# A decoder step on one core: convolved channels projected first, state scan beside the prompt projections, keys turned in place

## The chip, the core and the metric

One core of one Trainium2 chip runs the whole kernel. The metric is device time of one execution, in us. Seven units matter: TensorE (PE; its weight loads are shown as PEld), VectorE (DVE), ScalarE (ACT), GpSimd (POOL), SyncE (SP, which here only issues DMAs), and the 16 DMA engines. The program is written with explicit semaphores: each engine has one list of instructions, in program order, and waits where it is told to.

## The reference

One decoder layer, for 256 prompt tokens and for 32 sample tokens (8 batches of 4), all in float32:

```
h = rmsnorm(x); q | k | v | z | dt | x,B,C = h @ W_in          # 1024 -> 3080
q, k = rotated norms; attention: three dilated windows, combined   (prompt: own keys;
       samples: 640 of the 1024 cached keys and values per batch, and the new ones)
u = silu(conv4(x,B,C)); dt = softplus(dt + bias)
y = state-space scan over two chunks of 128 (samples: one chunk, start state from the cache)
x += [attention | rmsnorm(y * silu(z))] @ W_out
x += softmax(q_mem . k_mem) v_mem @ W_mo                       # 256 memory rows
x += top-4-of-32 experts, gated, 1024 -> 2048 -> 1024
```

Besides x, the step returns the new keys, values, convolution tails, scan states and memory keys and values.

## The kernel before

The weights go through `ring`, six slots of 128x4096 floats, in the order of the list `UNITS`; unit u uses slot u mod 6. SyncE walks the list, and before unit u waits until the unit six places earlier is used up (`wait_freed`). Cached keys and values are units too (K0 to K7, V0 to V7), as are the cached states (`h0`) and a scratch slot for their transposes. `arena` is a hand-laid scratch memory whose views (`XP`, `UT`, `QK`, `SS`, ...) overlap in time. PSUM has eight banks, named by number.

TensorE's list, which sets the order of everything (lines of the profile in brackets):

1. Turn the normed rows (L336); project q, k, v, z for two prompt tiles (L362: eight outputs, one bank each); the sample rows of all four (L369, four column groups side by side); dt (L377); x,B,C, eight blocks of 128 channels (L389). ScalarE copies each out of PSUM; VectorE norms and rotates q and k (`head_norm`, `rope`) and then convolves, ScalarE applies silu.
2. Turn q and k (L399, L407), the convolution tails (L415); prompt scores (L426); turn the convolved channels (`xb`, L454); running sums of dt (L443 to L448); turn the prompt's probabilities (L463) and weigh the values (L474).
3. The scan, for chunks 0 and 1 and the samples: scores and running sums (L511, L517), the cached states turned four at a time (L497), the carried part (L528, L538), the part within a chunk (L544), the chunk's state (L552). Between them VectorE builds the decay (L1198 to L1212) with an exponential on ScalarE (L1683). GpSimd multiplies the cached states by their decay (L1890). Then eight matmuls add to the cached states (L568), one at a time with VectorE (L1259), and y is turned (L582).
4. Window attention of the samples, for two groups of four batches. Each group goes as two pairs: turn 2x5 key tiles (L601; three PSUM banks, ScalarE copies them to `KTB`, L1699), scores of the pair (L622). After two pairs: max on VectorE, exponential on ScalarE (L1702), turn (L629), values (L642), then token selection (L648).
5. W_out projection (L662, L667) with the residual on VectorE; the memory rows normed and turned (L690); memory keys and values (L704); and so on through the memory attention, its projection, the router, and the experts (L872 to L945), which run in a loop of 16 pairs with their weights in the same ring plus one spare buffer (`SPARE`).

Around L704, w_mem_k is a ring unit; the rows that it multiplies are `HMT`, written by VectorE (L1331).

The first expert's units follow the front's last ones into their slots: `load_expert` (L2016), in the order of slots 0, 1, 2, 4, 5, spare, 3.

## Time and profile before

| | us |
|---|---|
| median of 3 runs | 1406.85 (1405.76 to 1408.14) |
| the profiled execution, by the same clock as the runs | 1409.51 |
| its span, first to last instruction | 1407.3 |
| PE busy | 1275.6 (91%) |
| DVE busy | 343.7 (24%) |
| ACT busy | 268.3 (19%) |
| POOL busy | 35.0 (2%) |
| DMA moved | 470.19 MB, mean 334 GB/s |

The profile is of one execution. Busy PE time is modelled and isn't PE at its peak; the granted clock (1.0 is full speed, 0.50 is half) stands beside it. Idle time of an engine counts only where another waits for it. The span is divided by the page into 40 slices of 35.2 us.

### The profile page before, as it was taken

The numbers are of one execution on the slowest core, as the hardware profiler recorded it, in microseconds if no ns is written. First come the engines' busy times: TensorE is split into PE (matmuls) and PEld (weight loads), VectorE is DVE, ScalarE is ACT, GpSimd is POOL, SyncE is SP. The second block draws the span as 40 slices with busy tenths as digits, with TensorE's granted clock in tenths as the row PEclk, the third lists the DMA queues.
The fourth block names the chain that finished last, engine by engine and source line by source line (L and its number), as shares of the span: only waits on it lengthen the run. The fifth ranks groups of instructions, "written<-read, shape, count | busy, mean of one in ns | idle before, by whom it ended". The sixth has DMA issues, their size and how long they took to land.

```text
span 1407.3 us, 15596 instructions
## 1 busy us (share of the span) xinstructions
PE 1275.6 (91%) x6333; PEld 519.7 (37%) x6333; DVE 343.7 (24%) x600; ACT 268.3 (19%) x520; POOL 35.0 (2%) x43
## 2 busy tenths in 40 slices
PE   6998788899778899999999999999999999999997
PEld 3467545344534233333323233232332323323232
DVE  1247550132405212212112121131211312113122
ACT  2126223310422110111102111021110211102111
POOL 0011320000000000000000000000000000000000
PEclk9998768999997899999999999999999999999999
DMA  9251028875028499999999999999999999999995
GB/s 343 103 198 49 0 78 317 312 268 203 12 74 344 154 409 432 426 431 426 431 426 431 426 430 427 430 427 430 427 430 427 430 427 431 426 430 427 430 427 217
DMA packets 54621, 470.19 MB, mean 334 GB/s; under 512 B 6417, under 2 KB 6673, under 8 KB 27972
## 3 DMA queue, kind: packets, MB, share of 16 engines
q1 hardware_dynamic: 52852, 463.69, 79.3%
q0 software_dynamic: 1744, 6.14, 1.4%
q8 instruction: 18, 0.29, 0.1%
q14 instruction: 7, 0.06, 0.0%
HBM read 463.94 MB, written 5.88 MB: 334 GB/s over the span
## 4 chain that ended last, share of the span: by engine, by line
PE 62%; DMA 23%; DVE 8%; ACT 6%; issue 1%; SPq 0%; ACTq 0%; DVEq 0%
DMA ring<-in_w_gate_up 23%; PE PS L913 22%; PE PS L945 10%; PE PS L893 5%; PE PS L362 4%; PE PS L662 3%; PE PS L389 2%; PE PS L704 2%; PE PS L622 1%; PE PS L716 1%; ACT arena L1699 1%; PE PS L642 1%; DVE arena L1503 1%; DVE arena L1505 1%; DVE arena L1500 1%
## 5 line engine op out<-in xcount | busy, mean ns | idle before, releaser
L913 PE MATMUL PS<-ring,arena 128*64 128x512 f32 x1792 | 406.2, 596 | 38.6 <-DMA ring<-in_w_gate_up 37.8
L913 PEld LDWEIGHTS PS<-ring,arena 128*64 128x64 f32 x1792 | 125.8, 137 | 307.1 <-issue 233.2
L945 PE MATMUL PS<-ring,arena 128*64 128x512 f32 x1024 | 230.3, 597 | 5.6 <-ACT arena L1817 5.6
L1500 DVE TENSOR_SCALAR arena<-PS 128x512 f32<-128x512 f32 x32 | 22.1, 692 | 425.9 <-PE PS L913 425.9
L1814 ACT ACTIVATE arena<-arena 128x512 f32<-128x512 f32 x32 | 20.1, 629 | 522.6 <-DVE arena L1500 522.6
L945 PEld LDWEIGHTS PS<-ring,arena 128*64 128x64 f32 x1024 | 69.3, 137 | 132.7 <-issue 118.8
L1466 DVE TENSOR_TENSOR X<-X,PS 128x1024 f32<-128x1024 f32 x34 | 41.5, 1221 | 272.2 <-PE PS L893 272.2
L872 PE MATMUL PS<-arena 128*64 128x512 f32 (+1 forms) x396 | 97.5, 610 | 2.2 <-issue 2.2
L893 PE MATMUL PS<-arena 128*64 128x512 f32 x340 | 81.3, 592 | 1.4 <-ACT arena L1824 1.4
L1824 ACT COPY arena<-PS 64x512 f32<-64x512 f32 x64 | 37.1, 580 | 158.5 <-PE PS L945 158.1
L362 PE MATMUL PS<-ring,arena 128*128 128x512 f32 x128 | 56.9, 607 | 1.1 <-DVE arena L1028 1.1
L913 PE MATMUL PS<-arena 128*64 128x512 f32 x256 | 57.6, 592 | 0.0
L872 PEld LDWEIGHTS PS<-arena 128*64 128x64 f32 (+1 forms) x396 | 25.7, 137 | 67.7 <-issue 67.7
L893 PEld LDWEIGHTS PS<-arena 128*64 128x64 f32 x340 | 24.4, 137 | 50.1 <-issue 50.1
L662 PE MATMUL PS<-ring,mixT 128*128 128x512 f32 x96 | 41.7, 594 | 0.0
L362 PEld LDWEIGHTS PS<-ring,arena 128*128 128x128 f32 x128 | 24.8, 194 | 32.5 <-issue 31.3
L837 PE MATMUL PS<-arena 32*64 32x512 f32 x264 | 36.8, 627 | 0.0
L1470 DVE TENSOR_TENSOR X<-PS,X 32x512 f32<-32x512 f32 x34 | 23.2, 682 | 49.4 <-PE PS L893 49.1
L389 PE MATMUL PS<-arena,ring 128*128 128x288 f32 x128 | 33.0, 422 | 0.0
L913 PEld LDWEIGHTS PS<-arena 128*64 128x64 f32 x256 | 18.4, 137 | 36.5 <-issue 36.5
L704 PE MATMUL PS<-ring,arena 128*128 128x512 f32 x64 | 27.7, 593 | 1.5 <-DVE arena L1331 1.5
L1796 ACT COPY arena<-PS 128x512 f32<-128x512 f32 x33 | 19.4, 587 | 47.8 <-PE PS L872 47.8
(325 smaller groups left out, 1028.4 us busy)
## 6 DMA issues: line engine op xcount, KB each, us to landing
ring<-in_w_gate_up SPq DMA_DIRECT2D x112, 2048.0 KB, 24.8
ring<-in_w_down SPq DMA_DIRECT2D x64, 2048.0 KB, 22.5
arena<-in_w_gate_up SPq DMA_DIRECT2D x16, 2048.0 KB, 27.6
ring<-in_w_in SPq DMA_DIRECT2D x6, 2048.0 KB, 17.0
ring<-in_cache_win_k SPq DMA_DIRECT2D x8, 1024.0 KB, 6.9
ring<-in_cache_win_v SPq DMA_DIRECT2D x8, 1024.0 KB, 10.4
ring<-in_w_out SPq DMA_DIRECT2D x2, 2048.0 KB, 13.7
ring<-in_cache_mem_k SPq DMA_DIRECT2D x4, 1024.0 KB, 7.8
```

Of the source, the lines that this page charges most:

```text
L362: last = mm(PS[:, 2 * g + t, :], hT[:, k, t * P:(t + 1) * P], w[:, k, :], start=k == 0, stop=k == KT - 1)
L389: last = mm(PS[:, bank, 0:NTOK], w[:, k, m % 4 * P:(m % 4 + 1) * P], hT[:, k, :], start=k == 0, stop=k == KT - 1)
L662: last = mm(PS[:, 2 * t + half, :], lhs[:, k, t * P:(t + 1) * P], w(k), start=k == 0, stop=k == nk - 1)
L704: last = mm(PS[:, MKV_BANKS[n], :], HMT[:, k, t * P:(t + 1) * P], w[:, k, :], start=k == 0, stop=k == KT - 1)
L837: last = mm(PS[64 * half:64 * half + 64, nb, :], EROW[r, :], BGU[r, half * 512:(half + 1) * 512], start=True, stop=False, tile_position=(N ...
L872: last = mm(PS[64 * half:64 * half + 64, 2, :], SEL[0:m, t, :], XN[0:m, t, half * 512:(half + 1) * 512], start=t == 0, stop=t == 2, tile_p ...
L893: last = mm(PS[64 * part:64 * part + 64, banks[half], :], SW[:, at:at + 64], YB[:, half, :], start=True, stop=True, tile_position=(0, 64 * ...
L913: last = mm(PS[64 * half:64 * half + 64, nb, :], XT[:, k, :], w[:, k % 2, c:c + 512], start=False, stop=k == KT - 1, tile_position=(0, 64 ...
L945: last = mm(PS[64 * half:64 * half + 64, 5, :], AT[:, k % 4, 64 * (k // 4):64 * (k // 4) + 64], w[:, k % 4, half * 512:(half + 1) * 512], ...
L1466: v.tensor_tensor(x, x, PS[0:n, b:b + 2, :], ALU.add).then_inc(sem("scatter_added"), 1)
L1500: v.tensor_scalar(G1.rearrange("q (c b p) -> q c b p", **by_part), gu[:, 0], 7.0, None, ALU.min).then_inc(sem("gate_ready"), 1)
L1824: ins = s.copy(YB[64 * odd:64 * odd + 64, half, :], PS[64 * half:64 * half + 64, 5, :])
```

## The change

It touches the front only (all before the expert loop). Six edits go together:

- **Order of projection.** x,B,C and dt come first, then the sample rows of q, k, v, z, then the eight prompt outputs in the order z0 z1 q0 k0 q1 k1 v0 v1 (`PROMPT_OUTS`), through two banks by turns. `project(i, k0, k1)` does part of one; the parts stand between steps of the scan.
- **The scan** runs before prompt attention and beside these parts. The cached states are turned one at a time through one bank (bank 7), each waiting for ScalarE's copy of the one before. `XD` is gone: dt multiplies `XB` in place, and `start_y` takes the skip term first. GpSimd builds all three `DTRI` before it scales the cached states.
- **Norms of q and k** (`norm_qk`) come after the scan on VectorE; eight state updates follow behind y.
- **Keys in place.** A turned key tile is copied back over the tile it came from; `KTB` is gone. Two banks by turns instead of three. The score matmuls read the four dense tiles of a batch with a stride. A group scores all four batches at once, one column group of 32 each: 48 matmuls a group for four batches.
- **Prompt attention and window attention overlap.** Twenty key tiles (batches 0 to 3) are turned between the steps of prompt attention; window attention's steps stand between the four W_out outputs of the prompt.
- **Loads.** `LOADS` gives SyncE's order, apart from the slots in `UNITS`. Values leave the ring: `VA` are four arena buffers, filled once the scan is over. K units are used up when their group's scores are done. The first expert's units go to slots 0 to 4, the spare, then 5.

```diff
+UNITS = ["z", "q", "k", "v", "xbc0", "xbc1",
+         "K0", "K1", "K2", "K3", "h0", "scratch",
+         "K4", "K5", "K6", "K7", "wout0", "wout1",
+         "wmq", "mem0", "mem1", "wmk", "mem3", "wmv",
+         "pad", "pad", "pad", "mem2", "pad", "wmo"]
+LOADS = ("xbc0 xbc1 z q k v h0 K0 K1 wout1 K2 K3 V0 V1 V2 V3 wout0 K4 K5 K6 K7 V4 V5 V6 V7 "
+         "wmk wmq mem0 mem1 wmv mem3 mem2 wmo").split()
...
+            def turn_state(b):
+                if b == 0:
+                    loaded("h0")
+                    pe.wait_ge(sem("proj_kept"), 3)
+                else:
+                    pe.wait_ge(sem("h0t_kept"), b)
+                for p in range(4):
+                    last = nc.tensor.transpose(PS[:, 7, p * P:(p + 1) * P], H0[:, b, p, :], ident)
+                last.then_inc(sem("h0_turned"), 1)
...
+            project(0, 0, KT)
+            turn_xb(0)
+            turn_xb(1)
...
+            project(1, 0, 4)
+            turn_xb(2)
+            project(1, 4, KT)
...
+            chunk_scores(0)
+            for c in range(4):
+                turn_state(c)
+                if c < 3:
+                    project(2, 2 * c, 2 * c + 2)
+            within(0)
+            chunk_state(0)
+            project(2, 6, KT)
+            chunk_scores(1)
+            for c in range(4):
+                turn_state(4 + c)
+                if c < 3:
+                    project(3, 2 * c, 2 * c + 2)
+            carried(1)
+            within(1)
+            chunk_state(1)
+            project(3, 6, KT)
+            chunk_scores(2)
+            project(4, 0, 5)
+            carried(2)
+            within(2)
+            project(4, 5, KT)
...
+            project(5, 0, KT)
...
+            project(6, 0, 4)
+            pe.wait_ge(sem("state_rows_kept"), 1)
+            turn_qk(0, (2, 3))
+            project(6, 4, KT)
+            project(7, 0, 4)
+            turn_y(0)
+            turn_y(1)
+            project(7, 4, 6)
+            turn_y(2)
+            add_states(0)
+            project(7, 6, KT)
+            add_states(1)
...
+            def turn_keys(n):
+                g, b, j = n // 20, n // 5, n % 5
...
+                if n % 20:
+                    pe.wait_ge(sem("kt_kept"), n - 1)
...
+            for n in range(10):
+                turn_keys(n)
+            turn_probs(0, (0, 1))
+            for n in range(10, 14):
+                turn_keys(n)
+            pe.wait_ge(sem("scores_kept"), 2)
+            weigh_values(0, 2)
+            turn_probs(1, (3, 6, 7, 0))
+            for n in range(14, 18):
+                turn_keys(n)
+            weigh_values(1, 1)
+            for n in range(18, 20):
+                turn_keys(n)
...
+            window_scores(0)
+            pe.wait_ge(sem("att_kept"), 2)
+            loaded("wout0")
+            project_half(mixT, 8, wout[0], 0, WOUT_BANKS[0][0], "mixed_ready")
+            turn_window_probs(0)
+            loaded("wout1")
+            project_half(mixT, 8, wout[1], 0, WOUT_BANKS[0][1], "mixed_ready")
+            weigh_window(0)
+            project_half(mixT, 8, wout[0], 1, WOUT_BANKS[1][0], "mixed_ready")
+            for n in range(20, 40):
+                turn_keys(n)
+            window_scores(1)
+            project_half(mixT, 8, wout[1], 1, WOUT_BANKS[1][1], "mixed_ready")
+            turn_window_probs(1)
+            weigh_window(1)
+            pe.wait_ge(sem("mix_ready"), 1)
+            project_samples(mixT, 8, wout, WOUT_BANKS[2][0], "mixed_ready")
```

ScalarE's list from the first projection copy to the end of prompt attention, whose order the prediction uses:

```diff
+            keep_projected(0)
+            keep_projected(1)
...
+                s.activation(Z[0:n, t, :], Z[0:n, t, :], ACT.Silu).then_inc(sem("z_silu_ready"), 1)
+            act.wait_ge(sem("acum_ready"), 1)
+            s.activation(TOE, DT1, ACT.Exp)
...
+            keep_state(0)
+            keep_state(1)
+            seg_exp(0)
+            keep_state(2)
+            keep_state(3)
+            keep_projected(2)
+            keep_state(4)
+            keep_state(5)
+            seg_exp(1)
+            keep_state(6)
+            keep_state(7)
...
+            for n in range(5):
+                keep_keys(n)
+            prompt_exp(0)
+            for n in range(5, 10):
+                keep_keys(n)
+            prompt_exp(1)
+            act.wait_ge(sem("window_stored"), 64)
+            keep_probs(0, (0, 1))
+            for n in range(10, 14):
+                keep_keys(n)
+            keep_att(0, 2)
+            keep_probs(1, (3, 6, 7, 0))
+            for n in range(14, 18):
+                keep_keys(n)
+            keep_att(1, 1)
+            for n in range(18, 20):
+                keep_keys(n)
```

SyncE's waits for the values:

```diff
+            for i, name in enumerate(LOADS):
+                if name == "V0":
+                    sp.wait_ge(sem("h_updated"), 8)
+                    sp.wait_ge(sem("y_turned_kept"), 3)
+                    sp.wait_ge(sem("qk_normed"), 3)
+                    sp.wait_ge(sem("prompt_state_stored"), 16)
+                elif name == "V4":
+                    sp.wait_ge(sem("att_rows_ready"), 1)
+                elif name[0] != "V" and U[name] >= RING:
+                    wait_freed(U[name])
```

## Rows read from the trace of the kernel before

**Rows 1.** The page's part 2: what the DMA engines moved, by slice of 35.2 us.

```profile
GB/s 343 103 198 49 0 78 317 312 268 203 12 74 344 154 409 432 426 431 426 431 426 431 426 430 427 430 427 430 427 430 427 430 427 431 426 430 427 430 427 217
```

**Rows 2.** Table by stage: window, its length, then busy us by engine, clock, DMA.

```profile
core 0: us, PE busy (x) PEld busy (x) DVE busy (x) ACT busy (x) POOL busy (x), PEclk, DMA share, GB/s
116.70:147.60 30.90, 22.83 (x175) 20.25 (x175) 23.15 (x42) 20.25 (x67) 6.49 (x10) 0.78 0.13 47
147.60:202.90 55.30, 42.66 (x180) 24.74 (x180) 36.73 (x46) 10.62 (x20) 19.79 (x11) 0.67 0.04 12
202.90:277.50 74.60, 61.20 (x477) 36.51 (x476) 6.60 (x18) 25.77 (x51) 0.00 (x0) 0.86 0.83 308
277.50:312.20 34.70, 33.26 (x146) 15.82 (x146) 7.66 (x15) 5.59 (x12) 0.95 (x1) 1.00 0.72 256
312.20:466.35 154.15, 124.44 (x604) 66.56 (x604) 50.07 (x109) 40.39 (x93) 3.04 (x5) 0.87 0.40 156
466.35:1407.30 940.95, 885.71 (x4356) 295.36 (x4356) 183.64 (x294) 137.50 (x224) 0.00 (x0) 1.00 0.97 414
450.00:475.00 25.00, 19.29 (x75) 7.88 (x73) 6.68 (x21) 4.34 (x6) 0.00 (x0) 0.66 0.02 7
```

**Rows 3.** The chain of waits: start, us, what.

```profile
312.23 27.70 PE PS L704 x64
...
709.48 24.83 DMA ring<-in_w_gate_up
```

**Rows 4.** Timeline of SyncE, 400 to 440 us: start, us, engine, line, tensors.

```profile
401.61 18.50 SPq L2016 DMA_DIRECT2D ring<-in_w_gate_up  x3
...
436.93 0.33 SPq L2016 DMA_DIRECT2D ring<-in_w_gate_up  x1
```

**Rows 5.** Table by stage, four us in the state updates.

```profile
188.00:192.00 4.00, 4.00 (x5) 1.44 (x5) 1.42 (x3) 1.84 (x3) 0.85 (x1) 0.50 0.11 34
```

**Rows 6.** Groups by line, PE, 15 to 313 us: busy, mean ns, idle before.

```profile
L362 PE MATMUL PS<-ring,arena 128*128 128x512 f32 x128 | 56.9, 607 | 1.1 <-DVE arena L1028 1.1
L389 PE MATMUL PS<-arena,ring 128*128 128x288 f32 x128 | 33.0, 422 | 0.0
...
L369 PE MATMUL PS<-ring,arena 128*32 128x512 f32 x64 | 7.1, 594 | 0.0
...
L474 PE MATMUL PS<-arena 128*64 128x128 f32 x48 | 6.1, 409 | 3.5 <-ACT arena L1659 3.5
L463 PE MATMUL PS<-CN,arena 128*128 128x128 f32 x24 | 4.5, 360 | 0.0
...
L377 PE MATMUL PS<-WDT,arena 128*128 128x8 f32 (+1 forms) x48 | 4.3, 230 | 0.0
```

**Rows 7.** Timelines of POOL and DVE around the scaling of the states.

```profile
165.96 9.33 POOL L1890 TENSOR_TENSOR ring<-ring,small 128x1024 f32<-128x1024 f32 x4 [13.97 <-PE PS L497]
...
155.06 0.68 DVE L1218 TENSOR_TENSOR arena<-arena,RP 128x512 f32<-128x512 f32 x1
...
168.86 2.38 DVE L1218 TENSOR_TENSOR arena<-arena,RP 128x512 f32<-128x512 f32 x1
```

**Rows 8.** Timelines of ACT and PE: copies of turned keys, and turns of memory keys.

```profile
252.80 4.99 ACT L1699 COPY arena<-PS 128x512 f32<-128x512 f32 x10 [5.43 <-PE PS L601]
...
385.95 1.04 PE L773 MATMUL PS<-CN,ring 128*128 128x128 f32 x8
387.27 1.15 PE L773 MATMUL PS<-CN,ring 128*128 128x128 f32 x8 [0.29 <-ACT arena L1770]
```

**Rows 9.** Groups by line and shape, ACT, 116 to 203 us: the prompt's exponentials.

```profile
L1650 ACT ACTIVATE arena<-arena,small 128x256 f32<-128x256 f32 x8 | 4.0, 495 | 1.5 <-DVE small L1148 1.5
...
L1650 ACT ACTIVATE arena<-arena,small 128x128 f32<-128x128 f32 x8 | 3.1, 388 | 0.4 <-DVE small L1148 0.4
```

**Rows 10.** Groups by line, PE, 203 to 313 us: window attention.

```profile
L601 PE MATMUL PS<-CN,ring 128*128 128x128 f32 x160 | 23.0, 311 | 0.0
L622 PE MATMUL PS<-arena 128*32 128x512 f32 (+2 forms) x192 | 19.0, 354 | 3.2 <-ACT arena L1699 3.2
L642 PE MATMUL PS<-ring,arena 128*32 128x512 f32 x80 | 12.5, 787 | 2.0 <-ACT arena L1707 2.0
```

More of the change, by code:

```diff
@@ L56, in slot_loads @@
 def slot_loads(upto, slot):
-    return sum({"s": 0, "p": 0, "K": 2, "V": 2, "m": 2}.get(UNITS[i][0], 1) for i in range(slot, upto, RING))
+    return sum({"s": 0, "p": 0, "K": 2, "m": 2}.get(UNITS[i][0], 1) for i in range(slot, upto, RING))
 def constants():
@@ new lines, in turn_qk @@
+            def turn_qk(t, banks):
+                pe.wait_ge(sem("qk_normed"), t + 2)
+                for j in range(2):
+                    for p in range(4):
+                        last = nc.tensor.transpose(PS[:, banks[j], p * P:(p + 1) * P],
+                                                   QK[:, t, j, 2 * p:2 * p + 2, :].rearrange("p h d -> p (h d)"),
+                                                   ident)
+                    last.then_inc(sem("qk_turned"), 1)
+            project(6, 0, 4)
@@ new lines, in _ @@
+            pe.wait_ge(sem("state_rows_kept"), 1)
[9 more added lines that the diff above has]
+            add_states(1)
+            add_states(2)
+            add_states(3)
+            pe.wait_ge(sem("proj_kept"), 11)
+            for j in range(2):
+                r = slice(32 * j, 32 * j + 32)
+                for p in range(4):
+                    last = nc.tensor.transpose(PS[:, j, p * NTS:(p + 1) * NTS],
+                                               QKS[r, 2 * p:2 * p + 2, :].rearrange("p h d -> p (h d)"),
+                                               ident[r, r])
@@ new lines, in turn_probs, with weigh_values @@
+            def turn_probs(i, banks):
+                pe.wait_ge(sem("probs_ready"), i + 1)
+                for j in range(i + 1):
+                    for s in range(8):
+                        last = nc.tensor.transpose(PS[:, banks[2 * j + s // 4], s % 4 * P:(s % 4 + 1) * P],
+                                                   SCO[i][s // 4][:, s % 4, j * P:(j + 1) * P], ident)
+                last.then_inc(sem("probs_turned"), 1)
+            def weigh_values(i, bank):
+                pe.wait_ge(sem("probs_kept"), i + 1)
+                for p in range(4):
+                    for e in range(2):
+                        h = 2 * p + e
+                        for j in range(i + 1):
+                            last = mm(PS[64 * e:64 * e + 64, bank, p * P:(p + 1) * P], V[:, j, h * DH:(h + 1) * DH],
+                                      PT[:, j, 4 * e + p, :], start=j == 0, stop=j == i)
+                last.then_inc(sem("att_ready"), 1)
@@ new lines, in _ @@
+            for c in (6, 7):
+                silu_conv(c, slice(0, SEQ), c + 1)
+            for c in range(8):
+                silu_conv(c, slice(SEQ, NTOK), 9)
+            act.wait_ge(sem("proj_ready"), 1)
+            s.copy(QKS[0:64].rearrange("p h d -> p (h d)"), PS[0:64, 7, :]).then_inc(sem("proj_kept"), 1)
+            s.copy(V[0:NTS, 2, :], PS[64:96, 7, :]).then_inc(sem("proj_kept"), 1)
+            s.copy(Z[0:NTS, 2, :], PS[96:128, 7, :]).then_inc(sem("proj_kept"), 1)
+            root_heads(64, AH, DH)
@@ new lines, in _, with keep_qk @@
+            s.copy(HOUT, PS[:, 2, :].rearrange("p (c n) -> p c n", c=4)).then_inc(sem("state_rows_kept"), 1)
+            act.wait_ge(sem("y_gated"), 3)
+            square_y(2)
+            root_heads(P, 2 * AH, DH)
+            act.wait_ge(sem("y_squared"), 3)
+            root(RS, SSQ, 512)
+            keep_projected(5)
+            root_heads(P, 2 * AH, DH)
+            def keep_qk(t, banks):
+                for j in range(2):
+                    act.wait_ge(sem("qk_turned"), 3 * t + j + 1)
+                    s.copy((qT, kT)[j][:, :, t * P:(t + 1) * P],
+                           PS[:, banks[j], :].rearrange("p (c n) -> p c n", c=4)).then_inc(sem("qk_kept"), 1)
@@ L1654, in _, with keep_probs @@
-            for i in range(2):
+            def keep_probs(i, banks):
                 act.wait_ge(sem("probs_turned"), i + 1)
-                banks = (2, 3, 5, 6)
                 for j in range(i + 1):
```

1022 lines of the change are left out of this document (493 added, 529 removed).

## The prediction

> **What bounds the kernel now.** I read the page's 40 slices first [rows 1]. From the fourteenth slice on the DMA engines move some 430 GB/s; before that they have long holes. Two regimes, then. The table by stage puts their border at 466.35 us, the first expert matmul [rows 2]: the expert stage takes 940.95 us with DMA 97% busy, the front 466 us. The chain of waits says who leads in the expert stage: from about 650 us on every pair of experts holds a wait of this form for its weights, thirteen of them up to 1380 us [rows 3]. That stage can only move as a whole. It loads into six ring slots and one spare, so its first loads wait for front tensors: SyncE issues them at 401.61 and the last before the first expert at 436.93 [rows 4], and DMA then stands idle (7 GB/s from 450 to 475 us [rows 2]) until the first expert gives slots back. So a us taken from the front is a us from the end, if the seven units still land before the first expert. Since DMA already idles there, front transfers aren't the bound either.
>
> In the front TensorE leads. Windows 116.7 to 202.9 us (prompt attention, then state scan) are the weak ones [rows 2]: 86.2 us, of which PE is busy 22.83+42.66 = 65.5, at granted clocks 0.78 and 0.67. So 20.7 us are idle, and the work at full clock is 22.83x0.78 + 42.66x0.67 = 46.4 us. The cause is a ping-pong of one short chain: PE waits for VectorE, ScalarE or GpSimd. The windows before it have a PE that never stops. The clock is at 1.2 GHz (0.50) for stretches that follow such gaps [rows 5].
>
> **The change, by stages.** The step everything hangs on is when the first memory projection (L704) starts: 312.2 us now [rows 3]. Nothing of consequence changes after it, so 154.15 + 940.95 us follow as before.
>
> *Stage 1, to the sample projections.* The order is now xbc, dt, samples; the six weight units come in the order xbc0, xbc1, z, q, k, v. 33.0 + 4.3 + 7.1 = 44.4 us from 15.6 [rows 6], ends 60.0. xbc1 is wanted 16.5 us after the start, where k was wanted after 13.7 without a wait. The dt weights move past z, q, k and v on SP's queue to stand right behind xbc1; they could be late by 0 to 3 us, taken 0. The convolution (VectorE) starts on arrival and is hidden by the 4.1 us that PE spends on each block.
>
> *Stage 2, state scan beside the prompt projections, to the first cached key.* PE work: 8 projections of 16 matmul instructions of 0.429 us, 6.87 each = 55 (from 56.9 for 128 [rows 6]). Besides, all of the 65.5 busy us of the two weak windows except the prompt's transposed probabilities and weighted values (4.5 + 6.1 [rows 6]), which belong to stage 3: 54.9 as they ran, or at full clock 46.4 less about 9, 37. Since projections now stand in most gaps, the clock stays mostly high: I take 45, nearer to full clock. That is 100. Waits, laid out instruction by instruction: PE comes to turn_state(1) before ScalarE has done z's silu and the exponentials (which stand behind the copy of projection 1): 1.5 us; turn_state(3) and within(0) stand behind seg_exp(0): 1.6; carried(1): 0.6; the tail of add_states about 1. The old stalls for VectorE in the scan are covered: chunk t's chain on VectorE and ScalarE (four steps on 128x1024 elements, each twice the size of the 0.68 us one in rows 7 and so about 1.2) is some 5 us, and between its matmuls stand 5 to 7 us of projection. VectorE's two long norms (norm_qk: four operations of that size, root and rotation, about 8 us each) have project 5 and 6 over the first, and the rest of 6 and of 7 over the second. 100 + 4 + 2 for clock drops = 106, bounds 96 (37 and 4) to 122 (54.9 and 12 of waits). Ends 166.
>
> GpSimd's scaling of the cached states (4 instructions, 9.33 us) moved behind the last dtri. The VectorE multiply of 0.68 us took 2.38 while it ran [rows 7]. Between the end of chunk 1 and within(2) PE has 1.7 + 1.3 + 4.3 + 3.3 = 10.6 us of its own; VectorE needs about 7, stretched. So cost 0; without cover up to 4. That the third dtri goes ahead of the scaling removes a wait of 2.3 us.
>
> The Trainium skill (SBUF — State Buffer, section "SBUF: two separate sides") has VectorE and GpSimd share one port pair under an exclusive lock, the loser blocked for the whole instruction. The trace agrees with the row above. By that rule the state scaling, four instructions beside chunk 1's VectorE chain, could stretch it by up to 9.3 us; if none of it were covered, the sum would be 9 us higher.
>
> *Stage 3, cached keys 0 to 19 among prompt scores.* All copies are ScalarE's, which leads here. Twenty key copies: 0.50 each with three banks (10 in 4.99), but 0.66 with two, as the memory keys show (two pairs start 1.32 us apart) [rows 8]. The change has two banks and writes a turned key tile back over itself: 13.2. Exponentials 8 x 0.388 + 8 x 0.495 = 7.1 [rows 9], with a table load and the reads of the sums about 8.5; eight further copies at about 0.5, 4.2. Sum 25.9; ScalarE's waits for PE's weighted values and VectorE's probabilities about 5; PE at half clock now and then (a key tile then takes 1.0 us, not 0.5) 2. Taken 33, bounds 26 and 40. Ends 199. The added waits on `window_stored` and `conv_stored` queue ScalarE's and VectorE's following copies behind GpSimd's stores, but those are issued some 10 us ahead: 0.
>
> *Stage 4, window attention among the w_out projections, to L704.* PE was busy 61.20 + 33.26 = 94.5 us from 202.9 to 312.2 [rows 2]. Off go twenty of the forty key turns, half of 23.0, and half of the scores' 19.0, since four batches go as one column group where two groups of two took 4 x 4.75 [rows 10]: 94.5 - 11.5 - 9.5 = 73.5. The twenty key turns left go from 11.5 to 13.3 at the two-bank pace: 75.3, and some 7 less if the 0.86 clock of the first window became 1.0. The waits for the window's exponential go (a projection stands there); those before the values (L642: 2.0 in two [rows 10]) stay, as do the like ones, 1.8, before the token matmuls, and 0.6 comes behind the last key. The end is longer than now: the memory rows' norm stood beside the w_out projections and now comes behind the last attention output (square, root, scale, turn, and the sample rows' four adds ahead of VectorE's copies): 2.6 us. Sum 82.3; taken 80, since more of it will run at full clock; bounds 75 and 90. If four-wide groups ran as two pairs, add 9.5; the value matmuls L642 already run four wide, ten streams of 512 columns in 12.5 us, so I don't expect it.
>
> DMA beside this: V0 to V3 wait on SP for the state update, and wout0, K4 to K7, V4 to V7 and the memory weights stand behind them. At 370 GB/s (308 at a share of 0.83 in the 202.9 to 277.5 window [rows 2]) 5.2 MB take 14 us. wout0 waits for the state store, lands about 190, wanted at 199; K4 to K7 are issued after the first scores at 204, land at 218, wanted at 233; V4 to V7 issued at 225, wanted at 265; w_mem_k, issued at 252, lands at 260, wanted at 279. None ends last. Which front tensor frees each slot changes, so the last expert unit is now a down-projection half, wanted later than gate-up part 3 was: 0.
>
> *Sum.* 60 + 106 + 33 + 80 = 279 for L704, against 312.2: 33 us less. Profiled execution: 1409.5 - 33 = 1376.5 (span 1407.3 - 33 = 1374.3). That execution was 2.7 us above the median of the runs, 1406.85, so the median after is 1374.
>
> **Rivals.** *A, as above*, with its own range 1364 to 1384. *B, PE holds 2.4 GHz and the waits are shorter*: stage sums at their low ends, 60 + 96 + 28 + 77 = 261, or up to 8 more; gain 43 to 51, time 1356 to 1364. For it: from 116.7 to 277.5 us busy time at a clock below 1.0 lost 5 + 14 + 9 = 28 us [rows 2]. Against: ScalarE leads stage 3 whatever PE's clock. *C, the interleave gives half back*: each projection piece is issued between waits in program order, so one late ScalarE instruction holds the projection as well. Ten waits of 1.5 us in place of five, and stages 3 and 4 near their ends (38, 87): gain 12 to 22, time 1385 to 1395. For it: ScalarE's list is strictly ordered and mixes state copies, exponentials and projections. *D, the front isn't worth its time*: weights late for the expert stage, gain under 3. Against: DMA idles before the first expert. Time 1405. *E, slower*: the mechanism is the clock. The new order replaces few long gaps by many of 0.6 to 1.6 us; if these hold PE at 1.2 GHz through stages 2 to 4, their work at full clock (about 92 + 15 + 68 = 175 us) doubles for the part concerned. Half clock for 43 us of work would eat the 33 us and the 10 us of slow clock that the sum contains; above that it's slower, and with 60 us of work at half clock the time is 1406.85 + 17 = 1424. The place would be the scan. For it: 0.67 in the scan now. Against: the 202.9 to 277.5 window has 0.86 with many gaps near 1 us already.
>
> **Chances.** A 0.62, B 0.13, C 0.18, D 0.03, E 0.04. The range with 8 in 10: 1360 to 1391. Measurement tells 0.2%, 2.8 us, from no change: faster 0.93, same 0.03, slower 0.04.
>
> **What would show it.** Right: L704 starts at 270 to 290 us; PE's gaps between 60 and 166 sum to 3 to 9 us and the clock there is above 0.9; the windows' score group is 9.5 us, not 19; the expert stage stays 941 us within 2; first sample projection ends about 60. Wrong: a PE wait over 3 us on ScalarE in the scan; a DMA as releaser anywhere before L704; key tiles above 0.8 us each; the clock below 0.75 between 60 and 166; the expert stage longer by what the front saved.

## The result, and the profile after

The changed kernel takes 1373.34 us (median of 1363.94 to 1375.52, four executions) where the kernel before takes 1406.7 in the same comparison (1405.76 to 1408.14): ratio 0.9749, 95% interval 0.9703 to 0.9795. Forecast were 1374.0 and a range of 1360 to 1391. The profiled execution took 1373.2 us, its span is 1371.2. One of the four was 9 to 12 us faster than the others; the last section comes back to it. One execution of serial_scan (1520.01 us, mean clock 0.825) and one of the kernel before beside it (2197.15 us, 0.554) fell in a slower state and are left out of the times and ratios below.

The table by stage of the changed kernel (window, length, busy us of each engine, clock, DMA), to be laid beside [rows 2]:

```profile
16.28:63.35 47.07, 47.07 (x241) 33.73 (x240) 18.49 (x45) 12.93 (x36) 2.93 (x11) 0.93 0.81 279
63.35:166.58 103.23, 99.96 (x414) 54.45 (x411) 63.21 (x102) 28.77 (x57) 25.40 (x20) 0.93 0.28 96
166.58:198.20 31.62, 20.80 (x155) 17.62 (x153) 9.03 (x13) 23.31 (x61) 0.72 (x1) 0.84 0.79 308
198.20:275.04 76.84, 69.34 (x540) 34.54 (x541) 13.58 (x31) 21.01 (x42) 0.95 (x1) 1.00 0.66 248
275.04:431.00 155.96, 126.80 (x603) 67.82 (x603) 49.88 (x109) 39.57 (x91) 3.03 (x5) 0.85 0.42 157
431.00:1371.20 940.20, 885.50 (x4356) 298.35 (x4356) 183.75 (x294) 137.91 (x225) 0.00 (x0) 1.00 0.98 414
```

Three things are to be seen. The last two rows are nearly those of before (154.15 and 940.95 us; the first expert matmul itself starts at 431.39, which makes them 156.35 and 939.8): whatever was gained was gained ahead of the memory projections (L796, formerly L704), which start at 275.04 instead of 312.23, 37.2 us earlier. Of that 36.1 reach the end of the span. The second row, the state scan with the prompt projections in it, has a PE that is busy 99.96 of 103.23 us; before, the two windows that held the scan and the prompt attention were busy 65.5 of 86.2. And of the four stages that the change rebuilt, the third leaves PE idle most: PE is busy 20.80 of its 31.62 us, ScalarE 23.31.

PE's waits in the second stage, as the view of waits sums them (from 63 to 166 us):

```profile
PE PS L492 <- ACT ring L1763: 2.3, 2, 1.6
PE PS L501 <- ACT ring L1763: 0.8, 1, 0.8
PE PS L524 <- DVE mixT L1306: 0.2, 1, 0.2
```

That is 3.3 us in four waits (in the fences, `PE PS L492 <- ACT ring L1763: 2.3, 2, 1.6` reads: line 492 of PE waited for ScalarE's line 1763, 2.3 us in two waits, the longest 1.6). The window attention's groups of the changed kernel, to be laid beside [rows 10] (PE, 198 to 275 us):

```profile
L652 PE MATMUL PS<-CN,ring 128*128 128x128 f32 x80 | 11.7, 284 | 1.5 <-ACT ring L1825 1.0
L706 PE MATMUL PS<-ring 128*32 128x512 f32 x64 | 7.3, 595 | 1.4 <-ACT ring L1825 1.4
...
L706 PE MATMUL PS<-ring 128*32 128x128 f32 x64 | 2.1, 272 | 0.0
```

With its third shape (1.0 us) L706, the scores of eight batches, is busy 10.4 us where L622 took 19.0. score_pairs, below, tests whether that comes of the four column groups.

### The profile page after: what moved, and what is told of

It reads as the page before. It is cut to its first block, busy times and chain, and to the rows that moved or that the text cites. A ratio compares the mean times of both kernels' runs of the same rounds, so it can differ in the third digit from the quotient of the medians.

```text
span 1371.2 us, 15591 instructions
## 1 busy us (share of the span) xinstructions
PE 1254.9 (92%) x6333; PEld 511.6 (37%) x6333; DVE 344.1 (25%) x606; ACT 270.2 (20%) x520; POOL 33.4 (2%) x43
## 4 chain that ended last, share of the span: by engine, by line
PE 63%; DMA 24%; ACT 6%; DVE 6%; issue 1%; SPq 0%; ACTq 0%; DVEq 0%
DMA ring<-in_w_gate_up 23%; PE PS L1004 23%; PE PS L1036 10%; PE PS L984 5%; PE PS L423 4%; PE PS L744 3%; PE PS L395 3%; PE PS L796 2%; PE PS L808 1%; PE PS L652 1%; DVE arena L1626 1%; DVE arena L1628 1%; DVE arena L1623 1%; PE PS L1025 1%; ACT arena L1989 1%
## 5 line engine op out<-in xcount | busy, mean ns | idle before, releaser
L1004 PE MATMUL PS<-ring,arena 128*64 128x512 f32 x1792 | 406.0, 596 | 35.2 <-DMA ring<-in_w_gate_up 34.4
L1999 ACT COPY arena<-PS 64x512 f32<-64x512 f32 x64 | 37.1, 580 | 159.6 <-PE PS L1036 159.3
L423 PE MATMUL PS<-ring,arena 128*128 128x512 f32 x128 | 58.1, 596 | 0.0
L395 PE MATMUL PS<-arena,ring 128*128 128x288 f32 x128 | 35.2, 441 | 0.0
L652 PE MATMUL PS<-CN,ring 128*128 128x128 f32 x160 | 24.6, 297 | 11.6 <-ACT ring L1825 11.0
L796 PE MATMUL PS<-ring,arena 128*128 128x512 f32 x64 | 29.4, 622 | 2.0 <-DVE arena L1454 2.0
```

Of the source, the lines that this page charges most:

```text
L395: last = mm(PS[:, XBC_BANKS[m], 0:NTOK], w[:, k, m % 4 * P:(m % 4 + 1) * P], hT[:, k, :], start=k == 0, stop=k == KT - 1)
L423: last = mm(PS[:, i % 2, :], hT[:, k, t * P:(t + 1) * P], w[:, k, :], start=k == 0, stop=k == KT - 1)
L652: last = nc.tensor.transpose(PS[:, KT_BANKS[g][n % 2], p * P:(p + 1) * P], K[:, j, p * P:(p + 1) * P], ident)
L796: last = mm(PS[:, MKV_BANKS[n], :], HMT[:, k, t * P:(t + 1) * P], w[:, k, :], start=k == 0, stop=k == KT - 1)
L1004: last = mm(PS[64 * half:64 * half + 64, nb, :], XT[:, k, :], w[:, k % 2, c:c + 512], start=False, stop=k == KT - 1, tile_position=(0, 64 ...
L1999: ins = s.copy(YB[64 * odd:64 * odd + 64, half, :], PS[64 * half:64 * half + 64, 5, :])
```

## Experiments

The same stretch of code is granted 2.4 GHz in some executions and 1.2 GHz in others (last section), and the changed kernel alone spreads over 14 us. So each experiment is read twice: by its ratio to the kernel before, and by the stage of its own profile that it touches. All stages in one table, us, each kernel from the one execution that was profiled; "tails" are the turned convolution tails (L413), the first score is L635, the first window score L706, the memory projections L796 in the changed kernel's lines:

| kernel | tails to first score | to first window score | to memory projections | to first expert | ratio to before, 95% |
|---|---|---|---|---|---|
| changed | 98.45 | 36.40 | 76.84 | 156.35 | 0.9749 (0.9703-0.9795) |
| changed_again | 97.98 | 37.50 | 76.84 | 159.57 | 0.9709 (0.9679-0.9739) |
| serial_scan | 122.57 | 35.37 | 76.86 | 157.20 | 0.9915 (0.9897-0.9933) |
| score_pairs | 98.45 | 36.46 | 87.65 | 153.07 | 0.9784 (0.9759-0.9808) |
| keys_last | 94.06 | 38.69 | 78.55 | 156.33 | 0.9746 (0.9724-0.9768) |
| wout_last | 94.08 | 33.90 | 88.55 | 155.47 | 0.9840 (0.9817-0.9863) |
| three_key_banks | 94.07 | 33.88 | 74.10 | 151.80 | 0.9693 (0.9663-0.9723) |
| states_spread | 105.75 | 36.19 | 77.40 | 151.76 | 0.9786 (0.9759-0.9814) |
| dt_spread | 98.55 | 36.29 | 77.40 | 152.35 | 0.9704 (0.9671-0.9737) |
| no_scaling | 98.36 | 36.83 | 77.39 | 152.40 | 0.9720 (0.9689-0.9752) |
| dve_copies | 98.16 | 36.17 | 79.10 | 151.39 | 0.9744 (0.9719-0.9769) |
| mem_first | 94.06 | 36.57 | 75.05 | 155.45 | 0.9719 (0.9686-0.9752) |
| best | 99.01 | 32.79 | 74.99 | 152.40 | 0.9695 (0.9670-0.9719) |

**serial_scan: the projections in a block ahead of the scan.**

```
             project(1, 4, KT)
+            for i in range(2, 8):
+                project(i, 0, KT)
...
             for c in range(4):
                 turn_state(c)
-                if c < 3:
-                    project(2, 2 * c, 2 * c + 2)
```

> The six projections that stand in pieces inside the state scan go ahead of it as one block, their copies and VectorE's two head norms beside them; the scan then runs alone. Theory (the gain is the filling of the scan's gaps): PE's waits in the scan come back. Per chunk VectorE's and ScalarE's four steps take about 5.5 us with one or two state turns left beside them, so about 3 us of wait for each of three chunks, 4 to 5 us for the norm of y behind the last, and some 8 us of half clock: 15 to 25 us more than the changed kernel, 1388 to 1398 us, with the clock in the scan below 0.85. Rival (the gain comes from the other stages and from convolving first, and the interleave is worth little): less than 5 us more, 1373 to 1378.

Measured: 1395.91 us, 22.6 above the changed kernel's first median and 29.5 above its second (changed_again, below). Its stage is 24.1 us longer than the profiled changed kernel's (28.5 longer than that of executions that had full clock there), the stages behind it are the same within 1.1 us. The table by stage of this kernel, and PE's waits in the stage:

```profile
61.87:184.44 122.57, 111.19 (x383) 61.34 (x379) 57.84 (x97) 31.57 (x60) 23.41 (x19) 0.80 0.21 74
```

```profile
PE PS L494 <- ACT ring L1751: 5.7, 6, 2.2
PE PS L578 <- DVE arena L1334: 3.1, 1, 3.1
PE PS L526 <- DVE mixT L1296: 1.1, 1, 1.1
```

The theory stands in its size and the rival falls, but the theory's parts don't: the waits are 11.4 us (with two of 0.8 and 0.7), only 8 more than with the interleave, where I had expected some 14. The larger part is the clock. The stage's mean is 0.80, and from 148 to 168 us, with the scan alone on PE, it is 0.50: busy 111.19 us for work that takes 90.8 us in the executions where the same stage is at 1.00, and 95.2 in the profiled changed kernel. So of the interleave's 28.5 us against an execution at full clock 20 are clock and 8 are waits; of the 24.1 against the profiled changed kernel, 16 and 8.

**score_pairs: a group of four batches as two pairs.**

```
-                for part in range(3):
+                for part, pair in [(part, pair) for pair in range(2) for part in range(3)]:
                     for p in range(4):
-                        for b in range(4):
+                        for b in (2 * pair, 2 * pair + 1):
```

> A score group of four batches is issued as two pairs, all else as in the changed kernel. Theory (four column strips stream at once, and nothing hides a group): each group goes from 4.8 to about 9.6 us, two groups, 9.6 us more in the stage of the window attention and at the end, 1383 us. Rival (a group of four is no faster than two pairs, or the longer group is hidden by waits that follow it): under 3 us more.

The window attention's stage is 87.65 us, 10.8 more than in the changed kernel and 10.2 more than the 77.4 of three other kernels with the same code there, and the scores' groups doubled (PE, 197 to 286 us):

```profile
L706 PE MATMUL PS<-ring 128*32 128x512 f32 x64 | 14.5, 595 | 1.4 <-ACT ring L1825 1.4
L706 PE MATMUL PS<-ring 128*32 128x128 f32 x64 | 4.2, 273 | 0.0
L706 PE MATMUL PS<-ring 128*32 128x32 f32 x64 | 1.7, 196 | 0.0
```

20.4 us for 10.4. Four column groups do stream at once: the gain over pairs is shown, 10.0 us here where 9.5 were forecast, and nothing hides it. The time itself (1377.96, executions from 1373.59 to 1382.18) is 5 us above the changed kernel's first median and 12 above its second. In the two profiled executions 8.3 us of difference are left, since the stage behind took 3.3 us less here (153.07 for 156.35), in code that is the same.

**keys_last: the first twenty key tiles behind the prompt attention.**

```
-            for n in range(10):
-                turn_keys(n)
             turn_probs(0, (0, 1))
...
             weigh_values(1, 1)
-            for n in range(18, 20):
+            for n in range(20):
                 turn_keys(n)
```

> The twenty key tiles of the first four batches are turned behind the prompt attention instead of among it, on TensorE and in ScalarE's copies. Theory (the turns fill waits of the prompt attention for VectorE and ScalarE): the stage of 31.6 us becomes about 25 us of prompt attention plus 20 x 0.66 = 13 us, 38 us, so 5 to 9 us more, 1378 to 1382. Rival (ScalarE bounds the stage by the sum of its work, whatever the order): 0 to 2 us more.

1372.83 us, ratio 0.9746: it falls between the changed kernel's two measurements. Its stage (first score to first window score) is 38.69 us; the profiled changed kernel has 36.40, and the three kernels with the same code in this stage and full clock ahead of it have 33.88 to 36.57. So 2 to 5 us. PE's waits from 156 to 196 us show why it isn't more:

```profile
PE PS L660 <- DVE ring L1382: 7.6, 1, 7.6
PE PS L670 <- ACT arena L1835: 3.9, 2, 2.1
```

11.5 us of waits for the attention's own chain come into the open, but the waits on key copies, 10.0 us in five in the changed kernel, are down to 1.0. That lies between the rival (0 to 2) and the theory (5 to 9): waits of one kind were changed for waits of the other. It doesn't show that the sum of ScalarE's work is the bound; dve_copies, below, speaks against that.

**wout_last: the output projection behind the window attention.**

```
             window_scores(0)
             pe.wait_ge(sem("att_kept"), 2)
-            loaded("wout0")
-            project_half(mixT, 8, wout[0], 0, WOUT_BANKS[0][0], "mixed_ready")
             turn_window_probs(0)
...
             weigh_window(1)
+            for t in range(2):
+                for half in range(2):
+                    loaded(f"wout{half}")
+                    project_half(mixT, 8, wout[half], t, WOUT_BANKS[t][half], "mixed_ready")
```

> The four prompt blocks of the output projection go behind the window attention of both groups instead of among it; the memory rows' norm then stands beside them. Theory (the projections fill the wait for each group's maximum and exponential, about 5 us each): 10 us of waits come back, the 2 us gap ahead of the memory projections and one ahead of the turns of the memory rows go: 5 to 9 us more, 1378 to 1382. Rival A (the clock): the longer gaps hold PE at half clock in the stage, 12 us or more. Rival B: what the interleave saves it gives back at the memory rows' norm, 0 to 2 us.

1385.96 us, 12.6 above the changed kernel's first median; the stage is 88.55 us, 11.7 more. Its waits (PE, 190 to 296 us) hold two of 3.3 and 3.2 us ahead of the turns of the probabilities (for the first of them the profile names no releaser, which it writes as "issue"):

```profile
PE PS L715 <- issue: 3.3, 1, 3.3
PE PS L715 <- ACT arena L1867: 3.2, 1, 3.2
PE PS L792 <- DVE arena L1449: 1.5, 1, 1.5
```

6.5 us of waits, not 10; the stage's clock is 0.92 where the changed kernel has 1.00, and PE is busy 74.69 us for 69.34. So 5.4 us of the 11.7 are clock again, 6.4 are waits, and rival A comes close (it wanted 12).

**three_key_banks: PSUM banks 0, 1 and 3 for key tiles 20 to 39.**

```
-        KT_BANKS = ((4, 5), (0, 1))
+        KT_BANKS = ((4, 5), (0, 1, 3))
...
-                    pe.wait_ge(sem("kt_kept"), n - 1)
+                    pe.wait_ge(sem("kt_kept"), n - 1 - g)
...
-                    last = nc.tensor.transpose(PS[:, KT_BANKS[g][n % 2], p * P:(p + 1) * P],
+                    last = nc.tensor.transpose(PS[:, KT_BANKS[g][n % 20 % (2 + g)], p * P:(p + 1) * P],
```

> The turned key tiles 20 to 39 go through three PSUM banks (0, 1, 3) instead of two, all else as in the changed kernel. Theory (with two banks each tile waits for the copy of the tile but one before it, 0.66 us a tile; with three ScalarE copies without a pause, 0.50 to 0.54): 20 tiles from 13.2 to 10.0-10.8 us, the window attention's stage 76.8 us to 73.6-74.4, the time 2.4 to 3.2 us less. Rival (ScalarE's copy and its semaphore bound the pace, whatever the banks): 0. The clock between 150 and 165 us, half in some executions and full in others, moves the whole by about 5 us, so the stage decides.

1365.76 us (1357.91 to 1368.96); the interval of its ratio overlaps those of both measurements of the changed kernel, so the stage decides. It is 74.10 us, 2.74 less than the changed kernel's, inside what was expected. The timeline of ScalarE shows the pace: copies in one unbroken run here (the window cuts it after sixteen), pairs with a pause in the changed kernel.

```profile
224.61 7.93 ACT L1825 COPY ring<-PS 128x512 f32<-128x512 f32 x16 [20.75 <-PE PS L652]
```

```profile
233.73 1.07 ACT L1825 COPY ring<-PS 128x512 f32<-128x512 f32 x2 [0.26 <-PE PS L652]
235.06 1.14 ACT L1825 COPY ring<-PS 128x512 f32<-128x512 f32 x2 [0.26 <-PE PS L652]
```

7.93/16 = 0.50 us a tile against 1.33/2 = 0.66; all twenty take 9.9 us for 13.2.

**states_spread: six of the eight state updates among the last projections.**

```
             turn_qk(0, (2, 3))
-            project(6, 4, KT)
+            add_states(0)
+            project(6, 4, 6)
+            add_states(1)
...
+            for n in range(4):
+                update_states(n)
+            norm_qk(1)
```

> Six of the eight 32-row state updates go from the end of the scan into the last two prompt projections, on TensorE and VectorE. Theory (in the changed kernel the eight updates, the small turns and the prompt scores follow each other, and the granted clock falls to 0.50 there while PE never pauses; between 128-row projections it does not): the clock stays 1.00 from 140 to 165 us in every execution, the prompt scores start at about 156.5 us in place of 161.8, 1368 us. Rival A (the fall has nothing to do with what PE runs there): 0.50 in some executions as before, time spread as before. Rival B (VectorE's second norm, now 3 us later, becomes what PE waits for): the scores start later, +1 to +3 us.

1378.63 us, 5 us above the changed kernel's first median and 12 above its second, more than rival B had: the first score stands 105.75 us behind the tails. PE's waits name it:

```profile
PE PS L585 <- DVE mixT L1367: 4.1, 1, 4.1
```

VectorE's second norm started at 147.53 instead of 135.55, since PE handed it the updates only every 3 us, and what stands behind the norm on VectorE (the copies of the turned y) was waited for. The clock was 0.50 from 160 to 170 us, in a stretch that begins behind that wait of 4.1 us. The theory of the clock isn't decided by this kernel: it added a gap of its own.

**dt_spread: the 24 matmuls of 8 columns in three portions.**

```
-                    for t in range(3):
-                        for k in range(KT):
...
+                if m in (4, 5, 6):
+                    t = m - 4
+                    for k in range(KT):
```

> The 24 matmuls of 8 columns (dt) stand 8 each before the xbc blocks 4, 5 and 6, not all before block 4. Theory (the 24 in a row of about 5 us make the clock fall to 0.5-0.6 behind them): no value below 0.9 between 33 and 48 us, the stage 16.3 to 56.4 shrinks by 2 to 3 us. Rival (the clock falls after them in any arrangement, or for another reason): 0, or three smaller falls. The softplus of dt comes one block later; the cumulative sums want it at 71 us, 10 us after it is there: 0.

The windows of four us show the clock (36 to 44 us, the changed kernel; 36 to 48, this one):

```profile
36.00:40.00 4.00, 4.00 (x29) 3.52 (x29) 0.42 (x3) 0.00 (x0) 0.00 (x0) 0.52 1.06 389
40.00:44.00 4.00, 4.00 (x12) 2.94 (x11) 0.00 (x0) 0.00 (x0) 0.00 (x0) 0.63 1.05 387
```

```profile
36.00:40.00 4.00, 4.00 (x26) 3.51 (x26) 1.36 (x4) 0.46 (x2) 0.21 (x1) 1.00 1.05 387
40.00:44.00 4.00, 4.00 (x30) 2.95 (x29) 0.45 (x1) 0.37 (x2) 0.00 (x0) 1.00 1.05 387
44.00:48.00 4.00, 4.00 (x22) 3.19 (x21) 2.14 (x7) 0.31 (x2) 0.21 (x1) 1.00 1.06 333
```

From the first dt matmul to the last xbc matmul are 20.06 us, here and in best, which contains the same edit; in the eleven profiles of kernels that have the 24 in a row they are 21.57 to 23.21 (changed kernel 23.14, from 33.27 to 56.41). So the portions save 1.5 to 3.1 us. The whole block of the projection, 35.68 us against 38.76 to 40.69, differs by more, but part of that lies in its first 64 matmuls, ahead of the edit: they take 15.79 us in some executions, this one among them, and 17.16 in the changed kernel's. All eleven have windows at half clock behind the dt matmuls; this kernel and best have none below 1.00 between 30 and 50 us. The kernel before has such a fall too, where its dt matmuls end (83.77 us; the view shows PE alone):

```profile
84.00:88.00 4.00, 4.00 (x11) 0.57 1.06 290
```

The time, 1367.33 us, agrees but doesn't prove it (its interval overlaps changed_again's).

**no_scaling: GpSimd's state scaling left out** (the sample rows' new states lack the decay of the old ones).

```
-                g_.tensor_tensor(H0[:, :, p, :], H0[:, :, p, :], bc(DECS[:, p, :], 2, NST),
-                                 ALU.mult).then_inc(sem("h0_scaled"), 1)
+                g_.tensor_copy(H0[:, 0, p, 0:1], H0[:, 0, p, 0:1]).then_inc(sem("h0_scaled"), 1)
```

> GpSimd's scaling of the cached states (4 multiplies, 8.35 us) is left out, so the sample rows' new states miss the decay of the old ones. Theory (VectorE's instructions beside it are stretched from 0.68 to 1.5-1.75 us, some 5 us in all, but projections cover them): the five VectorE instructions are short again, PE's waits and the time stay, within 1 us. Rival (one port pair under an exclusive lock, the lost time not covered): 4 to 9 us less.

The timelines of VectorE, the changed kernel and this one:

```profile
110.61 1.75 DVE L1322 TENSOR_TENSOR arena<-arena 128x512 f32<-128x512 f32 x1
113.12 1.54 DVE L1331 TENSOR_TENSOR arena<-arena,small 128x512 f32<-128x512 f32 x1
115.30 1.66 DVE L1338 TENSOR_TENSOR arena<-arena 128x512 f32<-128x512 f32 x1
```

```profile
110.52 0.69 DVE L1322 TENSOR_TENSOR arena<-arena 128x512 f32<-128x512 f32 x1
112.51 0.69 DVE L1331 TENSOR_TENSOR arena<-arena,small 128x512 f32<-128x512 f32 x1 [0.23 <-PE PS L533]
113.85 0.69 DVE L1338 TENSOR_TENSOR arena<-arena 128x512 f32<-128x512 f32 x1
```

The stretch comes from GpSimd's multiply, 2.9 us over these three (three instructions, where I had expected five and some 5 us); VectorE reaches the end of its list for chunk 1 2.4 us sooner; and PE's stage stays as it was (98.36 for 98.45 us). Instructions of VectorE that read PSUM beside the scaling (L1325, L1333) take 0.69 us either way. The cost of 0 for this step is shown, and the rival of 4 to 9 us is out.

**changed_again, dve_copies, mem_first, best.** The first is the changed kernel, unedited. dve_copies moves six of ScalarE's copies in the prompt attention to VectorE; mem_first:

```
             for t in range(2):
                 norm_rows(MP, t)
-            add_rows(0, 2, WOUT_BANKS)
...
                 ins.then_inc(sem("hm_kept"), 1)
+            add_rows(0, 2, WOUT_BANKS)
```

best holds both, three_key_banks, dt_spread, and ScalarE's copy of the first turned state ahead of its exponentials.

> The changed kernel itself, beside the three others on one chip. Its four earlier executions were three at 1373 to 1376 us and one at 1364. Theory (the clock between 150 and 165 us is full in some executions and half in others, worth 5 us, and likewise behind later gaps): a spread of 6 to 12 us, and the mean granted clock orders the times. Rival (the 1364 was a stray): all within 3 us of 1374.

> In the prompt attention VectorE takes two copies of the attention output and the four of the second block's turned probabilities from ScalarE, all else as in the changed kernel. Theory (with the key turns in it the stage is bound by ScalarE's list: putting the keys behind the attention cost 2.3 us of stage, not 7): six copies of 0.5 us leave it and PE waits less for it, the stage from first score to first window score 36.4 us less 3 to 4, at the end 1370 us. Rival (the stage is bound by the chain scores, exponentials, turned probabilities, values, and the copies lie in it on either engine): 0 to 1 us.

> VectorE's four adds of the sample rows go behind its copies of the turned memory rows, all else as in the changed kernel. Theory (the gap of 1.99 us ahead of the memory projections is these adds, and the 29.4 us of the projections in place of 27.7 is half clock behind the gap): gap 0.5 to 0.7 us, projections 27.7, together 3 us less, 1370.5 us. Rival (the gap is the norm of the memory rows): 0.

> Together: three key banks, the dt matmuls spread, VectorE's copies in the prompt attention, the memory rows' copies first, and ScalarE's copy of the first turned state ahead of its exponentials (PE's wait of 1.6 us goes). If they add up: 2.7 + 4.4 (both as measured by stage) + 3 + 3 + 1.6 = 14.7 us below the changed kernel, 1358.6 us. Rival (they overlap, and half clock elsewhere takes part of it back): 1362 to 1366.

changed_again: 1366.38 us, six executions, 1362.53 to 1377.07; the granted clocks order them, 0.981 and 0.979 (twice) for the three near 1363, 0.971 for 1369.07, 0.968 and 0.966 for 1375.12 and 1377.07. So the 1364 of the first comparison was no stray. dve_copies: its stage is 36.17 us where kernels with half clock in the stage before have 36.3 to 37.5, so the rival is right, though the time, 1370.05 us, is the theory's 1370. ScalarE's busy time fell by 3.2 us (20.14 for 23.31), PE's idle time by 1.1 (9.7 for 10.8), and PE's busy time rose by 0.9 at a clock of 0.74 for 0.80. So the sum of ScalarE's list isn't what bounds this stage; that the chain of scores, exponentials, probabilities and values is, was argued and not tested. mem_first: the wait ahead of the memory projections shrank from 2.0 to 0.2 us, and the stage was 75.05 us; 1368.47 us, an interval that overlaps changed_again's. The wait was VectorE's adds. That the half clock behind it was the wait's doing isn't shown, although the projections took 27.7 us in place of 29.4. The memory projections in the changed kernel, in no_scaling (the same order) and in mem_first:

```profile
275.04 29.40 PE L796 MATMUL PS<-ring,arena 128*128 128x512 f32 x64 [1.99 <-DVE arena L1454]
275.84 27.70 PE L796 MATMUL PS<-ring,arena 128*128 128x512 f32 x64 [1.40 <-DVE arena L1454]
267.22 27.70 PE L796 MATMUL PS<-ring,arena 128*128 128x512 f32 x64 [0.20 <-DVE arena L1453]
```

Four other kernels with the unedited order (three_key_banks, states_spread, dt_spread, dve_copies) have 1.40 and 27.70 as well. In those five it is the matmuls just ahead of the wait (L752) that take longer, 5.35 us for 3.66: the stretch at half clock falls ahead of the wait or behind it. In mem_first it fell at neither, in best, with the same edit, ahead again.

best: 1364.32 us (1360.21 to 1367.9), ratio 0.9695. Its rival is right: 9 us below the changed kernel's first median but 2 below its second, and not distinguishable from that or from three_key_banks by the intervals. Its theory also added up terms that were too large: 4.4 us for the dt matmuls, of which 1.5 to 3.1 are the edit's, and 3 for VectorE's copies, which bring no such gain. Two more reasons show in its profile: the first state's earlier copy only moved the wait (one of 2.8 us in place of 1.6 and 0.7), and the clock was 0.62 from 72 to 76 us, with no wait before it, and 0.52 from 92 to 96, behind the wait.

## Why the prediction was right, step by step

The sum held, 279 forecast and 275.0 measured for the memory projections, and so did case A, in its own range. That the median came within 0.7 us of 1374 is luck: the steps are off by +3.4, -2.8, -1.4 and -3.2 us and partly cancel, and the same kernel, measured again, had a median of 1366.38. By its steps:

*A us of the front is a us of the end.* Right. In all thirteen profiles of the table the time from the first expert to the end is 939.8 to 941.5 us, with first experts from 416.3 to 453.9 us. The weight transfers never decided, though in the fastest the front was 50 us shorter than before.

*Stage 1, 60.0:* measured 63.35. Begun 0.7 us later; the term "33.0 + 4.3 + 7.1" took the dt matmuls and the xbc blocks at the old pace, and they took 5.16 us for 4.3 and 35.2 for 33.0. Two things lie in that. Half clock behind the 24 short matmuls (dt_spread) cost 3.1 us here; the old kernel has the same fall, but shorter. And the first 64 xbc matmuls took 17.16 us where other executions have 15.79.

*Stage 2, 106:* measured 103.2, waits 3.3 where 4 to 5 were laid out, mostly at the places named: turn_state(1) 1.6, the second turn behind the exponentials 0.7 for the 1.6 forecast, carried(1) 0.8, nothing at the state updates. The norms of VectorE were covered. The work, forecast at 100 us, was 99.96 in the profiled execution, which had half clock from 152 us on, and 93.6 in three_key_banks at full clock; within it the projections took 58.1 where 55 were taken (the row that the prediction names has 56.9). What I hadn't weighed is how the gain of the interleave divides: not mostly filled gaps but mostly clock (serial_scan).

*Stage 3, 33:* measured 31.6. The two-bank pace of 0.66 us held; PE's waits for key copies are 10.0 us in five. ScalarE is busy 23.31 us for the 25.9 summed up and idle 8.3 for the 7 added. The sum came out, but its premise, that ScalarE leads here, isn't borne out: with 3.2 us taken off ScalarE the stage was 0.2 us shorter, at a clock of 0.74 for 0.80 (dve_copies). That the interleave as such bought little (2 to 5 us, keys_last) wasn't something the prediction priced.

*Stage 4, 80:* measured 76.8, at clock 1.00 throughout, which "more of it will run at full clock" undersold by 3 us. Score groups 10.4 us against 19.0, with 9.5 forecast (that it is the column groups is shown by score_pairs); twenty key tiles 13.2 for the 13.3 forecast (a third bank would have made them 9.9, three_key_banks); the gap ahead of the memory projections 2.0 in place of 2.6. The projections behind it took 29.4 us for 27.7 before, 1.7 us of half clock that no term held and whose cause stays open (mem_first).

*GpSimd's scaling, cost 0.* Right, shown by no_scaling. The stretch is there, 0.69 to 1.75 us on VectorE, and PE's projections cover it. Instructions with a PSUM source weren't stretched. The Trainium skill (SBUF — State Buffer, section "SBUF: two separate sides") describes an exclusive lock, for VectorE's instructions in a two-port mode or with two SBUF inputs; both observations agree with it. What it costs VectorE is no cost to a kernel whose PE isn't waiting for VectorE.

*Rivals.* Four of the ten executions of the changed kernel, 1362.5 to 1364 us, lie in B's 1356 to 1364, and three_key_banks, with full clock in stage 2, has 96.9 us there for B's 96, though 31.1 in stage 3 for its 28 (B called these stage sums the low ends; the low ends given were 26 and 75 for stages 3 and 4, not 28 and 77). No profile caught the changed kernel itself in such an execution. So B was given too little, or rather A and B are the same kernel with different grants of the clock. C (late ScalarE instructions) fell in the scan, with waits of 3.3 us; in stage 3 its waits are there, 10.0 us, but they were in the forecast's sum. D fell by the first step. E's mechanism is real, and it worked for the change: with the scan alone on PE, as in the old order, the clock is 0.50 for a stretch of 20 us (serial_scan).

What stays untested: no run puts the old order of projection (x,B,C and dt last) back into the changed kernel. The parts that were tested (24 to 28 us for the scan's interleave, 10 for the column groups, 12 for the output projections, 2 to 5 for the keys) add up to more than the 37.2 us gained, so they don't add; each is the worth of one part with all the others in place.

## What to carry to other kernels

Fill a latency-bound stage with matmuls that depend on nothing in it, and expect two gains: the gap's time and the clock of everything around; in the scan here the second was the larger (20 us against 8). When a few short matmuls must run, try them in portions between large ones (1.5 to 3.1 us here for 24 of 8 columns); cutting up the 32-row state updates the same way gained nothing, since it made VectorE late. Where one execution's profile is the basis, look for stages whose clock is neither 1.0 nor 0.5 throughout, and give the forecast both values, because the next execution may have the other.

## What the hardware showed that I had not expected

The granted clock falls to 1.2 GHz where the profile shows no pause of PE. From 149 to 162 us the changed kernel runs 32-row state updates and turns without a gap; two windows of it are the first two rows below. In three_key_banks the same instructions in the same order begin at 148.5 us and end at 156.5, at 1.00, the other two rows:

```profile
152.00:156.00 4.00, 4.00 (x19) 2.86 (x18) 0.75 (x2) 1.85 (x5) 0.87 (x2) 0.53 0.80 250
156.00:160.00 4.00, 4.00 (x6) 1.29 (x6) 1.37 (x2) 0.00 (x0) 0.00 (x0) 0.50 0.92 327
```

```profile
148.00:152.00 4.00, 4.00 (x19) 1.72 (x18) 1.85 (x3) 1.76 (x5) 3.36 (x5) 1.00 0.48 127
152.00:156.00 4.00, 4.00 (x15) 1.79 (x13) 1.81 (x4) 1.55 (x5) 0.00 (x0) 1.00 0.97 305
```

Of the ten profiles in which PE's code from the tails to the first score is the same, four were at full clock there (94.1 us from tails to first score) and six at half (98.0 to 98.6). Identical stretches also differed later: 151.4 to 159.6 us from the memory projections to the first expert. The mean granted clock orders the changed kernel's executions from 1362.53 to 1377.07 us (changed_again), so differences like these make up its spread of 14 us; the kernel before spread over 1402.6 to 1414.3 in the comparison beside three_key_banks. What decides between the two in one execution stays open; a transfer doesn't seem to, since DMA was as busy in one of the full-clock rows (0.97) as in the others. A step worth less than 3 us can't be told by times of five or six executions here, only by its stage, and even there only between profiles with the same clock.
